# First feed-forward block of a hybrid decoder step: fourteen tiles as paired block products, eight as plain tiles

## The chip, the cores and the metric

The kernel runs on one core of a Trainium2 chip. The metric is the device time of one execution in microseconds; 520 token columns (512 prompt positions and 8 new tokens) go through the whole trunk in one launch. TensorE (PE) multiplies, ScalarE (ACT), VectorE (DVE) and GpSimd (POOL) work on the data around it, SyncE (SP) issues most of the transfers.

## The reference, cut to what matters

The trunk has two layers. Each adds half a SwiGLU feed-forward block, then a mixer, then half a feed-forward block again. The mixer of layer 0 is a diagonal state-space layer (S5), that of layer 1 a latent attention.

```
D_MODEL = 1024; SEQ = 512; DEC_BATCH = 8; D_FF = 2816; FFN_RES = 0.5
def swiglu(x, w_gate, w_up, w_down):
    return (jax.nn.silu(x @ w_gate) * (x @ w_up)) @ w_down
x = x + FFN_RES * swiglu(rmsnorm(x, ffn_norm[layer, 0]), ffn_w_gate[layer, 0], ffn_w_up[layer, 0], ffn_w_down[layer, 0])
...
    dt = jnp.exp(log_dt)[:, None]; mag = jnp.exp(dt * a_re)          # S5: lambda, B and C from parameters alone
    lam_re, lam_im = mag * jnp.cos(dt * a_im), mag * jnp.sin(dt * a_im)
    ...                                                              # powers of lambda times B and C feed the scan
```

The change is in the very first feed-forward block (called ffn00) and in the preparation of the S5 parameters, which runs beside it.

## The kernel before, in words

Activations lie transposed: 8 blocks of 128 channels by 520 columns. Every fp32 operand is split into a high and a low fp32r part (`wh`, `wl` for weights, `xh`, `xl` for the input), and a product takes three passes: high by high, low by high, high by low. A matrix instruction has 260 columns, so a weight block of 128x128 costs six instructions. The 2816 hidden features are 22 tiles of 128.

**ffn00** is written plainly (`ffn_first` on each engine). Eleven tiles are done: for each tile a gate product and an up product (`product`, line 2377; 8 channel blocks, 48 instructions each), evicted by DVE with the row scale (lines 1903 and 1907), gated with ACT's sigmoid and two DVE multiplications, and split into `h0` by ACT (L1218) and DVE (L1914). Then eight down products over these 11 tiles (66 instructions each) are added to `x` by DVE (L1924). Then the same again for the other eleven tiles, "half 1". Each weight slot is loaded by SP (`load`, L762) into one of two buffers `raw`, copied to `wh` by ACT (`his`, L990), and the rest taken by DVE (`los`, L1579). A load of slot n is issued once `los` of slot n-2 is done. Each queue takes its work strictly in the order written.

**The other three feed-forward blocks** (`seven` on each engine, planned by class `Seven`) do four tiles plainly and the other eighteen in pairs. A pair of tiles against two halves of the channels and two halves of the columns is a 2x2 block product, done with seven products in place of eight (L2487; each is 12 instructions for gate and 12 for up, so 168 for a pair, against 192 for its two tiles done plainly). It needs sums of weight blocks (DVE, L1680 to L1697), sums of input blocks (`xof`, split into `xoh`, `xol`), and extra copies out of and into PSUM by ACT. The pairs lie in groups `GROUPS = ((0,1,2,3),(4,5,6,7),(8,9,10))`; after each group come eight down products over its tiles (`down`, L2459), which need the last pair's hidden values in order (`z_hl`).

**The S5 preparation** lies beside ffn00. Lambda is made by POOL at the start. PE spreads it over channels with `param_rows` after tile 3, `b_rows` (matrix instructions and turns) after tile 10, `c_columns` in the first down products. DVE then does `lambda_columns` (L1946) and `input_matrix` (L1955 to L1959) at the first down product of half 0, one `input_power` (L1969 to L1973) in each of tiles 12 to 18, and one `output_power` (L1992 to L2001) in each of the last down products. After the last input power (`s_bp`) POOL makes powers of lambda (`mu`, L3390 to L3408), writes zeros to DRAM (L3417, waits until they have landed) and, once ACT has written `bp` to DRAM (L1229, 4 MB, at the first down product of half 1), gathers it back turned as `wsh` (L3422, 4 MB, 512-byte pieces). SP, in order behind its weight loads, loads the carried state (L828, four small transfers); PE turns it after the sixth of the last eight down products and waits for it there (`s_s0`). `wsh` is first read some 7 us after the block ends (L2771).

Of the kernel before, what the change touches and what calls it, by code (L numbers as in the profile page):

```python
# [27 lines left out]
P = 128  # L28
# [72 lines left out]
TOGETHER = NF // 2 - PLAIN  # L101
# [5 lines left out]
NSS = len(S_STEPS)  # L107
AFTER_CH = 2 * NPG * (R + DR) - (NQT + 2 * RT) * TOK
# [60 lines left out]
def plan():  # L169
    s = Slots()  # L170

    for _ in range(2):
# [19 lines left out]

class Seven:


    def __init__(self, then):
        self.kind, self.load, self.done, self.loads = [], [], [], []
        self.start, self.down = {}, {}
        for c, group in enumerate(GROUPS):
            for p in group:  # L200
                self.start[p] = len(self.kind)
                if p < PLAIN:
                    for f in (2 * p, 2 * p + 1):
# [32 lines left out]
    def counts(self):  # L236

        r, k = TOGETHER, len(self.loads)
        return {"in": (self.landed(k - 1 if (k - 1) % 2 == 0 else k - 2), self.landed(k - 1 if (k - 1) % 2 else k - 2)),
                "hi": self.n, "lo": self.n, "used": self.done[-1], "up": KD * (len(GROUPS) - 1),  # L240
                "xh": 7, "xl": 7, "xf": 5, "ev": 4 * PLAIN, "ps": 2 * PLAIN, "ph": 2 * PLAIN, "hh": NF // 2, "hl": NF,
# [15 lines left out]
def yoco_step(nc, inp, out):  # L257
    slots = plan()
    total = len(slots.nk)
    SEV = {"ffn01": Seven(True), "ffn10": Seven(True), "ffn11": Seven(False)}  # L260
    at = slots.at
    AFTER = {"ffn01": at["kv"], "ffn10": at["dq"], "ffn11": total}
    ctx = ExitStack()
    with ctx:
# [34 lines left out]
        with ExitStack() as s:  # L299
            bp, tmpc, lamc = take(s, ("bp", [P, KD, L, 2, NS], F32), ("tmpc", [P, 2, 2, KD * NS], F32),  # L300
                                  ("lamc", [P, 2, KD, NS], F32))
            with ExitStack() as a:
                xin, xsin, grow = take(a, ("xin", [P, 4, D], F32), ("xsin", [NB, D], F32),
                                       ("grow", [P, P], F32))
            with ExitStack() as a:
                h0, = take(a, ("h0", [P, 2 * HF, TOK], F32R))
# [59 lines left out]
        sums_at = {"ffn01": (sum_1, sum_2), "ffn10": (sum_1, sum_3), "ffn11": (sum_1, sum_2)}  # L366
# [22 lines left out]
        bnat = tmpc[:, 0].rearrange("p r (n c) -> p r n c", c=GC)  # L389
        lam, lam_l, fac = prm(8, 2), prm(2, 2), prm(10, 2)  # L390
        lam_r, lam_i, fac_r, fac_i = (prm(8 + i) for i in range(4))
        hfirst = (h0[:, 0:HF, :], h0[:, HF:2 * HF, :])

        def plane(j):
# [4 lines left out]
            ("s5_u_rows", (KD, P // GC, GC, L, NCH)), ("s5_w_rows", (KD, P // GC, GC, L, 2 * NS))))  # L399
        dr_us, dr_k = (nc.dram_tensor(n, shape, F32).ap() for n, shape in (  # L400
# [75 lines left out]
        r_out, R_0 = [s_in, p_in], [64, 48]  # L476
# [4 lines left out]
        z_in, IN_0 = x_in[0:2], 16  # L481
        z_hi, z_lo, z_used, z_up, z_xh, z_xl, z_xf = s_u, s_z, s_w, s_y1, s_yp, s_ysp, s_ct
        z_ev, z_ps, z_ph, z_hh, z_hl, z_sum, z_add = s_ls, s_bb, s_bp, s_sn, s_tp, s_e, s_xe
        z_seed, z_p5, z_u2, z_sg, z_h = s_ctc, s_sb, s_wb, s_x, s_sc
        now = {"hi": 8, "lo": 2, "used": 4, "up": 1, "xh": 4, "xl": 1, "xf": 2, "ev": 1, "ps": 1, "ph": 1, "hh": 2, "hl": 4, "sum": 11,
               "add": 9, "seed": 8, "p5": 2, "u2": 1, "sg": 16, "h": 8, "in": (IN_0, IN_0)}
        ZB = {}
        for f_, sv_ in SEV.items():
# [7 lines left out]
        HID = {"ffn00": 0, "ffn01": NF, "ffn10": 2 * NF, "ffn11": 3 * NF}  # L496
# [4 lines left out]
        NEXT = {"ffn01": "kv", "ffn10": "mla"}  # L501
        XN = {"glu": 0}
# [25 lines left out]
        def raw_of(name, n):  # L528
# [3 lines left out]
            if sv.kind[n][0] == "down":  # L532
                _, c, d = sv.kind[n]
                k = 2 * len(GROUPS[c])
# [21 lines left out]
        def as_slot(name, buf, n):  # L556
# [4 lines left out]
            k = KD if kind[0] == "plain" else 2 * len(GROUPS[kind[1]])  # L561
# [16 lines left out]
        def hid(name, c):  # L578

            if c == LAST and name in NEXT:  # L580
                return [t[:, 0:len(GROUPS[c])].rearrange("p i k t -> p (i k t)").rearrange("p (f c) -> p f c", c=TOK) for t in (xoh, xol)]
            return xh, xl

        PREPARE = {"ffn01": {2: 1, 3: 2, 4: 3, 5: 4}, "ffn10": {0: 1, 1: 2, 3: 3, 4: 4}, "ffn11": {2: 1, 3: 2, 4: 3, 5: 4}}
# [2907 lines left out]
```

## Time and profile before

| | |
|---|---|
| median of 3 runs | 2012.95 us (2010.68 to 2013.16) |
| span of the profiled execution | 2007.1 us |
| PE busy | 1960.4 us (98%), 17604 instructions |
| DVE busy | 1277.0 us (64%) |
| ACT busy | 820.4 us (41%) |
| POOL busy | 132.8 us (7%) |
| DMA | 211.55 MB, mean 105 GB/s |
| ffn00, first matrix instruction to the last update of x | 12.0 to 418.7 us |
| S5 mixer to its first output product | 418.7 to 481 us |

The profile shows one execution. The median of the timed runs is 5.85 us above its span; sums are made on the span and carried over to the median by that distance. Times are microseconds from the start of the span. In the page's 40 slices of 50 us PE is at 8 or 9 tenths throughout, the granted TensorE clock at 9 tenths or more.

### The profile page before, as it was taken

To read this page: it belongs to the slowest core of one execution; us is meant where nothing else is said; L and a number is where in the kernel's file an instruction comes from. 1 tells how busy PE (TensorE), PEld (TensorE's weight loads), DVE (VectorE), ACT (ScalarE), POOL (GpSimd) and SP (SyncE) were. 2 spreads that over 40 slices of the span, in tenths; PEclk is the share of its full clock that TensorE was granted. 3 is DMA by queue.
4 is the path that set the end of the run, shared out by engine and by line. 5 is a ranking of instruction groups with operands and counts; after the bars stand their busy time and mean duration, and the time that the engine had idled before them with its cause. 6 is when DMAs were issued, how large, how long until landed. Compare 5 with 4: busy or idle time off the path is not lost.

```text
span 2007.1 us, 41612 instructions
## 1 busy us (share of the span) xinstructions
PE 1960.4 (98%) x17604; PEld 1875.2 (93%) x17604; DVE 1277.0 (64%) x1771; ACT 820.4 (41%) x1243; POOL 132.8 (7%) x231
## 2 busy tenths in 40 slices
PE   8999999988999999999999999999989999999999
PEld 7999999987999999999999999997666799999998
DVE  6445486697469577576884856655764349668474
ACT  5332233343245244255452534454654244345252
POOL 3002002010000000000000000000047000000000
PEclk9999999989999999999999999999999999999999
DMA  7233234864342322234322322231248422323222
GB/s 151 84 102 88 75 93 115 269 140 100 95 137 85 120 89 95 77 105 116 97 85 85 127 85 86 84 101 51 54 119 231 149 71 83 127 85 120 91 74 75
DMA packets 260624, 211.55 MB, mean 105 GB/s; under 512 B 42372, under 2 KB 235426, under 8 KB 260450
## 3 DMA queue, kind: packets, MB, share of 16 engines
q1 hardware_dynamic: 248528, 187.52, 31.9%
q0 software_dynamic: 6656, 13.69, 2.4%
q10 hardware_dynamic: 5266, 7.85, 1.2%
q8 instruction: 130, 2.13, 0.4%
q14 instruction: 44, 0.36, 0.1%
HBM read 195.29 MB, written 10.33 MB: 102 GB/s over the span
## 4 chain that ended last, share of the span: by engine, by line
PE 67%; DVE 3%; ACT 2%; issue 2%; SPq 1%; DMA 1%; DVEq 0%; ACTq 0%
PE ps L2459 25%; PE ps L2487 25%; PE ps L2388 6%; PE ps L2401 2%; PE ps L2947 1%; PE ps L3053 1%; PE ps L3209 1%; PE ps L3086 1%; SPq L654 1%; SPq L639 1%; DMA cb<-cache_ckv 1%; PE ps L2841 1%; PE ps L3030 1%; DVE wl L1668 0%; DVE xl L1619 0%
## 5 line engine op out<-in xcount | busy, mean ns | idle before, releaser
L2388 PE MATMUL ps<-xh,wh 128*128 128x260 f32 x1088 | 286.9, 285 | 2.6 <-DVE xl L1619 1.4
L2388 PE MATMUL ps<-xl,wh 128*128 128x260 f32 x1088 | 283.7, 283 | 0.0
L2487 PE MATMUL ps<-xoh,wh 128*128 128x260 f32 x992 | 281.3, 284 | 1.3 <-DVE sq L1835 1.3
L2487 PE MATMUL ps<-xoh,wl 128*128 128x260 f32 x992 | 281.0, 283 | 0.0
L2487 PE MATMUL ps<-xol,wh 128*128 128x260 f32 x992 | 280.6, 283 | 0.0
L2459 PE MATMUL ps<-xh,wh 128*128 128x260 f32 x872 | 228.8, 284 | 0.6 <-DVE wl L1668 0.6
L1067 ACT ACTIVATE wh<-rw 128x1024 fp32r<-128x1024 f32 (+1 forms) x135 | 138.8, 1029 | 218.6 <-PE ps L2459 151.7
L2459 PE MATMUL ps<-xl,wh 128*128 128x260 f32 x872 | 227.0, 282 | 0.0
L2388 PE MATMUL ps<-xh,wl 128*128 128x260 f32 x1088 | 219.3, 283 | 0.0
L990 ACT ACTIVATE wh<-raw 128x1024 fp32r<-128x1024 f32 (+1 forms) x90 | 100.4, 1116 | 283.4 <-PE ps L2388 250.5
L2388 PEld LDWEIGHTS ps<-xh,wh 128*128 128x128 f32 x1088 | 205.6, 189 | 6.9 <-issue 3.9
L2388 PEld LDWEIGHTS ps<-xl,wh 128*128 128x128 f32 x1088 | 205.1, 188 | 0.0
L1668 DVE TENSOR_TENSOR wl<-rw,wh 128x1024 fp32r<-128x1024 f32 (+1 forms) x135 | 160.3, 1188 | 67.3 <-ACT wh L1067 67.2
L2487 PE MATMUL ps<-xoh,third 128*128 128x260 f32 x1040 | 198.6, 283 | 0.6 <-DVE sq L1835 0.6
L2487 PEld LDWEIGHTS ps<-xoh,wh 128*128 128x128 f32 x992 | 186.6, 188 | 1.6 <-DVE wl L1668 1.6
L2487 PEld LDWEIGHTS ps<-xol,wh 128*128 128x128 f32 x992 | 186.9, 188 | 0.0
L2487 PEld LDWEIGHTS ps<-xoh,wl 128*128 128x128 f32 x992 | 186.8, 188 | 0.0
L1579 DVE TENSOR_TENSOR wl<-raw,wh 128x1024 fp32r<-128x1024 f32 (+1 forms) x92 | 120.5, 1310 | 89.5 <-ACT wh L990 81.8
L2459 PE MATMUL ps<-xh,wl 128*128 128x260 f32 x872 | 175.5, 283 | 0.0
L2388 PEld LDWEIGHTS ps<-xh,wl 128*128 128x128 f32 x1088 | 167.9, 189 | 0.0
L2459 PEld LDWEIGHTS ps<-xh,wh 128*128 128x128 f32 x872 | 164.4, 189 | 1.7 <-DVE wl L1668 1.1
L2487 PEld LDWEIGHTS ps<-xoh,third 128*128 128x128 f32 x1040 | 164.8, 188 | 0.8 <-DVE third L1668 0.8
(550 smaller groups left out, 4202.2 us busy)
## 6 DMA issues: line engine op xcount, KB each, us to landing
rw<-ffn_w_gate SPq DMA_DIRECT2D x33, 1024.0 KB, 5.4
rw<-ffn_w_up SPq DMA_DIRECT2D x33, 1024.0 KB, 8.0
rw<-ffn_w_down SPq DMA_DIRECT2D x12, 2048.0 KB, 7.8
raw<-ffn_w_gate SPq DMA_DIRECT2D x22, 512.0 KB, 3.9
raw<-ffn_w_up SPq DMA_DIRECT2D x22, 512.0 KB, 3.9
raw<-ffn_w_down SPq DMA_DIRECT2D x16, 704.0 KB, 4.8
rw<-ffn_w_down SPq DMA_DIRECT2D x6, 1536.0 KB, 6.7
cb<-cache_ckv SPq DMA_DIRECT2D x72, 128.0 KB, 3.7
```

What stands on the lines that cost most here:

```text
L639: eng.dma_start(kb[j][:, g, :], inp["cache_kpe"][bass.ds(numbers[b][g], 1)].rearrange("a p r -> p (a r)")).then_inc(arrived[j], 16)
L654: eng.dma_start(cb[j][:, g, :], inp["cache_ckv"][bass.ds(numbers[b][g], 1)].rearrange("a p r -> p (a r)")).then_inc(arrived[j], 16)
L990: run(wh[par_][:, 0:size], raw[par_][:, 0:size], ACT.Copy).then_inc(w_hi, 1)
L1067: run(as_slot(name, slot_h(name, n), n), raw_of(name, n), ACT.Copy).then_inc(z_hi, 1)
L1579: tt(wl[par_][:, 0:size], raw[par_][:, 0:size], wh[par_][:, 0:size], ALU.subtract).then_inc(w_lo, 1)
L1668: tt(as_slot(name, slot_l(name, n), n), raw_of(name, n), as_slot(name, slot_h(name, n), n), ALU.subtract).then_inc(z_lo, 1)
L2388: got = mm(ps[0:width, bank + half, 0:HALF], w[par_][:, k * width:k * width + width], src[:, k0 + k, half * HALF:half * HALF + HALF], star ...
L2401: return nc.tensor.transpose(dst, src, ident[0:rows, 0:rows])
L2459: got = mm(ps[:, bank + half, T0], w[:, cols], src_[:, k, half * HALF:half * HALF + HALF], start=first and m == 0 and s == 0, stop=last an ...
L2487: got = mm(ps[:, bank + mat, T0], w[:, cols], src[:, j, k, :], start=first and k == 0 and m == 0 and s == 0, stop=k == 3 and m == 1, skip_ ...
L2841: got = mm(ps[:, bank + half, 0:HALF], w[slot][:, k * P:k * P + P], src[:, k, half * HALF:half * HALF + HALF], start=k == 0 and m == 0 and ...
L2947: got = mm(ps[:, 2 * (i % 2) + half, 0:HALF], cols, src[:, k, half * HALF:half * HALF + HALF], start=k == 0 and o == 0 and s == 0, stop=k ...
```

## The change

Only ffn00 and the S5 preparation change. Its first fourteen tiles now go through `seven`: tile 0 as before (`opening`), tiles 1 to 3 plainly, tiles 4 to 13 as five pairs in groups `((0,1,2),(3,4),(5,6))`, each followed by its eight down products. The last eight tiles (`SINGLE`) stay plain, with one set of eight down products. The hidden values of the first two groups are kept in `xh`, `xl`, where the input was; so POOL writes both to DRAM at the start and reads them back after the second group. That block has semaphores of its own (`ZS`, borrowed from later stages, which then wait for a count higher by `ONCE`).

The S5 preparation moves: `param_rows` into the third group's down products, `b_rows` between the gate and the up product of the first plain tile, `lambda_columns` and `input_matrix` into that tile on DVE, `input_power(f)` into plain tiles 1 to 7, `c_columns` after the third plain tile. The order in the last eight down products is as it was, with 8 tiles (48 instructions, 512 KB of weights each) where there were 11 (66 instructions, 704 KB).

```
-        for _ in range(2 * HF):
-            s.add("ffn00", KD)
-        for _ in range(KD):
-            s.add("ffn00", HF)
+    for _ in range(2 * (1 + SINGLE)):
+        s.add("ffn00", KD)
+    for _ in range(KD):
+        s.add("ffn00", SINGLE)
...
+GROUPS_FIRST = ((0, 1, 2), (3, 4), (5, 6))
+SINGLE = NF - 2 * sum(len(g) for g in GROUPS_FIRST)
...
+    SEV = {"ffn00": Seven(True, GROUPS_FIRST, 1), "ffn01": Seven(True), "ffn10": Seven(True), "ffn11": Seven(False)}
...
+            pool.wait_ge(xl_rdy, GEN["ffn00"] + KD)
+            for t, dst in zip((xh, xl), dr_x):
+                pool.dma_start(dst, t[:, :, :]).then_inc(x_kept, 16)
+            pool.wait_ge(x_kept, 32)
+            pool.wait_ge(ZS["ffn00"].used, ZB["ffn00"]["used"] + SEV["ffn00"].done[SEV["ffn00"].down[LAST - 1] + KD - 1])
+            for t, src in zip((xh, xl), dr_x):
+                pool.dma_start(t[:, :, :], src).then_inc(x_kept, 16)
...
+                seven("ffn00")
+                los(3)
+                for f in range(SINGLE):
+                    n, j = 2 + 2 * f, f % 2
+                    dve.wait_ge(w_used, n + 1)
+                    tt(halves(ta[:, j, :]), banks(0), halves(rbc[:, :]), ALU.mult).then_inc(f_g, 1)
+                    los(n + 2)
+                    if f == 0:
+                        lambda_columns()
+                        input_matrix()
+                    dve.wait_ge(w_used, n + 2)
...
+                    if f >= 1:
+                        input_power(f)
...
+                seven("ffn00")
+                pe.wait_ge(x_kept, 64)
+                pe.wait_ge(s_z, 1)
+                for f in range(SINGLE):
+                    n = 2 + 2 * f
+                    if f > 0:
+                        pe.wait_ge(f_g, f)
+                    product(n, 0, KD, X, 0)
+                    if f == 0:
+                        pe.wait_ge(x_upd, UPD["half"] + KD)
+                        b_rows()
+                    else:
+                        pe.wait_ge(f_u, f)
+                    product(n + 1, 1, KD, X, 2)
+                    if f == 2:
+                        c_columns()
```

The order on DVE where `lambda_columns` (`lst`) and `input_matrix` (`tmpc`, `bp`) stand. Before, behind the last tile of half 0 and ahead of the first update of `x`:

```order
L1914 TENSOR_TENSOR h<-ta,h 128x520 [waits f_hi]
L1946 TENSOR_SCALAR lst<-ps 64x32 [waits s5_param_ps]
L1946 TENSOR_SCALAR lst<-ps 64x32 x19
L1955 TENSOR_TENSOR tmpc<-bp,ps 128x1024 [waits s5_param_sb]
L1955 TENSOR_TENSOR tmpc<-bp,ps 128x1024
L1958 TENSOR_TENSOR bp<-tmpc 128x8x64 [waits s5_bb]
L1959 TENSOR_TENSOR bp<-tmpc 128x8x64
L1924 SCALAR_TENSOR_TENSOR x<-ps,x 128x520 [waits w_used,dch]
```

Now, in the first plain tile, between the eviction of its gate (`ta<-ps`) and that of its up product (`sq<-ps`):

```order
L1935 TENSOR_TENSOR ta<-ps,rbc 128x520 [waits w_used]
L1605 TENSOR_TENSOR wl<-raw,wh 128x1024 [waits w_hi]
L1979 TENSOR_SCALAR lst<-ps 64x32 [waits s5_param_ps]
L1979 TENSOR_SCALAR lst<-ps 64x32 x19
L1988 TENSOR_TENSOR tmpc<-fac_rows,ps 128x1024 [waits s5_param_sb]
L1988 TENSOR_TENSOR tmpc<-fac_rows,ps 128x1024
L1991 TENSOR_TENSOR bp<-tmpc 128x8x64 [waits s5_bb]
L1992 TENSOR_TENSOR bp<-tmpc 128x8x64
L1941 TENSOR_TENSOR sq<-ps,rbc 128x520 [waits w_used,dch]
L1943 TENSOR_TENSOR ta<-ta,tb 128x520 [waits f_sig]
L1945 TENSOR_TENSOR ta<-ta,sq 128x520 [waits f_t]
L1605 TENSOR_TENSOR wl<-raw,wh 128x1024 [waits w_hi]
```

The up product's eviction and the next up weights' low part now stand behind the whole of it.

The end of the block on DVE. Before, three tiles without a power lay between the last input power (lines 1969 to 1973) and the first update; the last tile ended so:

```order
L1911 TENSOR_TENSOR ta<-ta,sq 128x520 [waits f_t]
L1579 TENSOR_TENSOR wl<-raw,wh 128x1408 [waits w_hi]
L1914 TENSOR_TENSOR h<-ta,h 128x520 [waits f_hi]
L1924 SCALAR_TENSOR_TENSOR x<-ps,x 128x520 [waits w_used]
L1579 TENSOR_TENSOR wl<-raw,wh 128x1408 [waits w_hi]
L1992 TENSOR_TENSOR tmpc<-lst,cT 128x512 [waits s5_param_sb]
```

Now the last input power stands right ahead of the first update:

```order
L1948 TENSOR_TENSOR h<-ta,h 128x520 [waits f_hi]
L2002 TENSOR_TENSOR tmpc<-lamc,bp 128x1024 [waits s5_param_ps]
L2003 TENSOR_TENSOR tmpc<-lamc,bp 128x512
L2004 TENSOR_TENSOR tmpc<-lamc,bp 128x512
L2005 TENSOR_TENSOR bp<-tmpc 128x8x64 [waits dch]
L2006 TENSOR_TENSOR bp<-tmpc 128x8x64
L1955 SCALAR_TENSOR_TENSOR x<-ps,x 128x520 [waits w_used]
L1605 TENSOR_TENSOR wl<-raw,wh 128x1024 [waits w_hi]
L2025 TENSOR_TENSOR tmpc<-lst,cT 128x512 [waits s5_param_sb,s5_bp]
```

All that waits for it (`s5_bp`: the 4 MB write by ACT, POOL's powers and its gather) starts beside the down products and no longer three tiles ahead of them.

On SP the end of the block keeps its order (weights of the down products, then the carried state); only the weights are smaller:

```order
L771 DMA raw<-ffn_w_down 128x8x128 [waits w_lo] x8
L844 DMA tb<-state_s_re 128x128 [waits f_lo]
L844 DMA tb<-state_s_re 128x128
L844 DMA tb<-state_s_im 128x128 x2
L771 DMA raw<-s_w_glu_v 128x8x128 [waits w_lo]
```

## Rows read from the trace of the kernel before

**Rows 1.** The page, busy time of each engine: us, share of the span, instructions.

```profile
PE 1960.4 (98%) x17604; PEld 1875.2 (93%) x17604; DVE 1277.0 (64%) x1771; ACT 820.4 (41%) x1243; POOL 132.8 (7%) x231
```

**Rows 2.** Waits of PE from 30 to 370 us: total, times, longest.

```profile
PE ps L2414 <- DVE rstd L1605: 0.5, 1, 0.5
```

**Rows 3.** Chain that ended last: start, length, what, instructions; second feed-forward block.

```profile
664.71 46.03 PE ps L2459 x384
710.75 81.03 PE ps L2487 x672
```

**Rows 4.** Waits of PE from 571 to 700 us.

```profile
PE ps L2487 <- DVE sq L1835: 0.6, 1, 0.6
```

**Rows 5.** Timeline of DVE at the end of a group, second block: start, length.

```profile
898.74 0.42 DVE L1747 SCALAR_TENSOR_TENSOR sq<-ps,sq 128x260 f32<-128x260 f32 x1
...
900.30 1.31 DVE L1704 TENSOR_TENSOR xol<-sq,xoh 128x520 fp32r<-128x520 f32 x2 [1.14 <-ACT xoh L1085]
```

**Rows 6.** Timeline of ACT at the same place.

```profile
899.19 1.07 ACT L1085 ACTIVATE xoh<-sq 128x1040 fp32r<-128x1040 f32 x1 [1.64 <-DVE sq L1747]
```

**Rows 7.** Timeline of PE, `b_rows`, first and last of its 38 instructions.

```profile
153.53 1.89 PE L2710 MATMUL ps<-cst,be 128*128 128x64 f32 x16
...
157.14 0.52 PE L2401 MATMUL ps<-cst,cT 64*64 64x64 f32 x6
```

**Rows 8.** Timeline of DVE there: `lambda_columns`, end of `input_matrix`, next weights.

```profile
157.83 2.54 DVE L1946 TENSOR_SCALAR lst<-ps 64x32 f32<-64x32 f32 x20
...
167.57 0.70 DVE L1924 SCALAR_TENSOR_TENSOR x<-ps,x 128x520 f32<-128x520 f32 x1
168.19 2.61 DVE L1579 TENSOR_TENSOR wl<-raw,wh 128x1408 fp32r<-128x1408 f32 x1
```

**Rows 9.** Timeline of DVE, tile with the last power to the block's end.

```profile
315.11 0.70 DVE L1907 TENSOR_TENSOR sq<-ps,rbc 128x520 f32<-128x520 f32 x1 [2.19 <-PE ps L2388]
...
321.88 0.69 DVE L1973 TENSOR_TENSOR bp<-tmpc 128x512 f32<-128x512 f32 x1
...
349.63 0.70 DVE L1907 TENSOR_TENSOR sq<-ps,rbc 128x520 f32<-128x520 f32 x1 [2.65 <-PE ps L2388]
...
360.58 1.29 DVE L1992 TENSOR_TENSOR tmpc<-lst,cT 128x512 f32<-128x512 f32 x2
...
363.71 0.69 DVE L2001 TENSOR_TENSOR ctcw<-tmpc 128x512 f32<-128x512 f32 x1
...
418.04 0.70 DVE L1924 SCALAR_TENSOR_TENSOR x<-ps,x 128x520 f32<-128x520 f32 x1
```

**Rows 10.** Timeline of POOL: start chain's end, powers' start, zeros, gather.

```profile
42.87 0.28 POOL L3355 TENSOR_TENSOR cT<-cT 64x64 f32<-64x64 f32 x1
...
322.63 0.29 POOL L3390 COPY mu<-lst 128x128 f32<-128x128 f32 x1 [147.20 <-DVE bp L1973]
...
337.61 1.01 POOL L3417 DMA_DIRECT2D s_tap_rows<-kpT  x1 [0.30 <-POOL kpT L3415]
...
371.39 2.76 POOL L3422 DMA_DIRECT2D wsh<-s_w_rows  x1 [32.77 <-DMA s_w_rows<-bp]
```

**Rows 11.** DMA issues at 334 to 345, 360 to 368, 368 to 376: size, us to landing.

```profile
s_tap_rows<-kpT POOLq DMA_DIRECT2D x1, 448.0 KB, 3.9
...
raw<-ffn_w_down SPq DMA_DIRECT2D x1, 704.0 KB, 14.2
...
wsh<-s_w_rows POOLq DMA_DIRECT2D x1, 4096.0 KB, 23.3
```

**Rows 12.** Tile `raw` from 340 to 425 us: landing times of the down weights.

```profile
DMA to landing us min/median/max: 4.6/5.0/18.2
```

**Rows 13.** Timeline of SP: a down load, then the carried state.

```profile
377.97 0.37 SPq L762 DMA_DIRECT2D raw<-ffn_w_down  x1
...
385.98 9.42 SPq L828 DMA_DIRECT2D tb<-state_s_re  x2
...
395.44 0.91 SPq L828 DMA_DIRECT2D tb<-state_s_im  x2
```

**Rows 14.** Timeline of PE: the turns of the carried state.

```profile
399.24 0.66 PE L2401 MATMUL ps<-cst,tb 128*128 128x128 f32 x4
```

More of the change, by code:

```diff
@@ L12 @@
 import math
+from collections import namedtuple
 from contextlib import ExitStack
@@ L190, in plan, with __init__ @@
     return s
+Signals = namedtuple("Signals", "arrived hi lo used up xh xl xf ev ps ph hh hl sum add seed p5 u2 sg h")
 class Seven:
-    def __init__(self, then):
+    def __init__(self, then, groups=GROUPS, before=0):
         self.kind, self.load, self.done, self.loads = [], [], [], []
         self.start, self.down = {}, {}
-        for c, group in enumerate(GROUPS):
+        self.groups, self.pairs, self.skip = groups, sum(len(g) for g in groups), 2 * before
+        self.tiles = {p: [f for f in (2 * p, 2 * p + 1) if f >= before] for p in range(PLAIN)}
+        for c, group in enumerate(groups):
             for p in group:
@@ L202, in __init__ @@
                 if p < PLAIN:
-                    for f in (2 * p, 2 * p + 1):
+                    for f in self.tiles[p]:
                         for mat in range(2):
@@ L1744, in left_over @@
-                    tt(g[:, :, T1_], g[:, :, T1_], u, ALU.mult).then_inc(z_h, 1)
-                    dve.wait_ge(z_sg, Z["sg"] + 3 * r + 3)
-                    dve.wait_ge(z_used, Z["used"] + sv.done[sv.start[p] + 6])
-                    stt(g[:, 1, T0], ps[:, C_B + 1, T0], -1.0, g[:, 1, T0], ALU.mult, ALU.mult).then_inc(z_h, 1)
-                begins = {sv.start[p]: p for p in range(PLAIN + 1, NF // 2)}
+                    dve.wait_ge(z.sg, Z["sg"] + 3 * r + 2)
+                    dve.wait_ge(z.add, Z["add"] + 4 * r + 4)
@@ L1751, in ahead @@
+                    tt(g[:, :, T1_], g[:, :, T1_], u, ALU.mult).then_inc(z.h, 1)
+                    dve.wait_ge(z.sg, Z["sg"] + 3 * r + 3)
+                    dve.wait_ge(z.used, Z["used"] + sv.done[sv.start[p] + 6])
+                    stt(g[:, 1, T0], ps[:, C_B + 1, T0], -1.0, g[:, 1, T0], ALU.mult, ALU.mult).then_inc(z.h, 1)
+                begins = {sv.start[p]: p for p in range(PLAIN + 1, sv.pairs)}
                 def ahead(n):
@@ L1756, in ahead @@
                         second_sum(begins[n + 3])
-                seven_lo(name, 1)
+                if not sv.skip:
+                    seven_lo(name, 1)
                 if name in NORM:
-                    rms_row(name, lambda: seven_lo(name, 2))
-                for c, group in enumerate(GROUPS):
-                    apart = c == LAST and name in NEXT
+                    rms_row(name, lambda: seven_lo(name, 2 - sv.skip))
+                for c, group in enumerate(sv.groups):
+                    apart = c == LAST and name in APART
                     for p in group:
@@ L1868, in seven @@
                             los(AFTER[name])
+                        if apart and name not in NEXT:
+                            continue
                         if apart:
@@ L2477, in plain @@
                             each(k)
-                    got.then_inc(z_used, 1)
+                    got.then_inc(z.used, 1)
                 def seventh(p, j, mat, bank, first):
@@ L2501, in down @@
                             result(d - 1)
-                    got.then_inc(z_used, 1)
+                    got.then_inc(z.used, 1)
                 def result(d):
```

645 lines of the change are left out of this document (312 added, 333 removed).

## The prediction

> **What bounds the kernel now.** I read the page first: PE is busy for 1960.4 of 2007.1 us [rows 1], so only fewer matrix instructions, or PE standing idle somewhere new, can move the time. Then the waits of PE: from 30 to 370 us, nearly the whole first block, it waits 0.5 us in all [rows 2]. The first block is therefore a pure stream of matrix instructions, and every instruction less counts fully until some other engine or a transfer is late. Third, the chain through the second block, which already works in pairs: 384 plain instructions take 46.03 us and 672 paired ones 81.03 us [rows 3], so 0.1199 us a plain and 0.1206 us a paired instruction. Last, I looked for what is nearly late at the end of the block, since there the same S5 work is now to lie beside a third less matrix work.
>
> **Part 1, fewer instructions.** Five pairs are 5 x 168 = 840 paired instructions in place of 960 plain ones: 840 x 0.1206 - 960 x 0.1199 = 101.3 - 115.1 = **-13.8 us**. The down products are 22 x 48 = 1056 instructions either way, however they are grouped.
>
> **Part 2, entering the pairs.** The second block waits 0.6 us once for DVE's additions there [rows 4]; the same code runs here: **+0.6**, between 0 and 2.
>
> **Part 3, short groups.** The third instruction block of a group's first down product needs the hidden values of the last pair. After the last paired instruction DVE starts its multiplication at 898.74 [rows 5], ACT's copy runs from 899.19 to 900.26 [rows 6], DVE's rest of the first half is ready about 0.7 us after 900.30 [rows 5]: 2.4 us after 898.57, where that group's instructions ended (the multiplication starts 0.17 us later). A group of three tile pairs has 4 x 6 instructions, 2.9 us, ahead of that need, so it is hidden; the two groups of two pairs have 2 x 6, 1.4 us. That is 1.0 us each, **+2.0** (0 to 4). In those groups a down product is 24 instructions, 2.9 us; ACT's and DVE's copies for it are half the size of those in 5.75 us, so they fit.
>
> **Part 4, the parameters in the first plain tile.** `b_rows` takes PE 153.53 to 157.66, 4.1 us [rows 7], before and after, so nothing. But DVE's `lambda_columns` and `input_matrix` take 157.83 to 167.57, 9.7 us [rows 8]. Before, they lay beside a 7.9 us down product that nobody hurried. Now PE has the up product and the next gate product ahead, 96 x 0.1199 = 11.5 us from the end of `b_rows`, until it needs the next up weights, whose low part stands behind all that on DVE. From the end of `b_rows`: 10.0 us, then eviction and two multiplications at 0.7 each, then the low part, 1.2 us and up to 1 more, since the one in this place took 2.61 us against the 1.6 us of its kind while POOL worked [rows 8]. That is 14.5 us, so PE waits 3.0: **+3.0** (1 to 5). The later tiles have 11.5 us for about 10.3 of DVE, as now; the backlog is worked off in two tiles.
>
> **Part 5, keeping the input.** POOL issues the write of 4.26 MB when its parameter chain ends at 43.2 [rows 10]; ACT wants it done when the plain tiles end, near 27 + 7.3 products of 5.75 = 69 us. A 4.19 MB gather in 512-byte pieces took 23.3 us on the same queue [rows 11]; in long rows it can't be slower, so it lands by 67. The read back has the whole third group, 63 us of PE. Cost 0; if the write were late, up to 5 us.
>
> **Part 6, the end of the block.** Call D the start of the last eight down products (349.6 before [rows 9]). Before, the tail from D to the last update of x, 418.7 [rows 9], was 69.1 us, of it 528 x 0.1199 = 63.3 us of matrix work. Now it has 384 instructions, 46.0 us. DVE has less slack: its last power ends 7.4 us after the up product's end (315.1 to 322.6 [rows 9]), so its list starts at D + 7.4; then 8 x (0.7 + 1.2) for updates and weights, seven output powers at 3.8 (360.58 to 364.40 [rows 9]) and 2.7 for the last half power: 52 us. One stall comes on top: the weights of the fifth down product are requested at D + 9.4, just as ACT's 4 MB write runs; the load in that place took 14.2 us to land [rows 11] against 5.0 usually [rows 12], here about 12.6 (smaller), which holds DVE for 3 us, of which it had used up 0 to 2. So the last update ends near D + 53.5: an overhead over the matrix work of 7.5 us where it was 5.8: **+1.7** (0 to 5).
>
> Sum: -13.8 + 0.6 + 2.0 + 3.0 + 1.7 = **-6.5 us**. The profiled execution would have a span of 2000.6, the median 2012.95 - 6.5 = 2006.5 us. Adding up the ends of these terms gives -13 to +2.
>
> **Rival 1: the carried state comes behind the gather, and the kernel is slower.** SP loads the carried state behind the down weights, PE waits for it after the sixth down product. Before, POOL issued its 4 MB gather at 371.39 [rows 10], D + 21.8, and it landed 23.3 us later, at 394.7 [rows 11]. A down load issued at 377.97 [rows 13], behind it, landed only 18.2 us later [rows 12], at 396.2; SP was held for 9 us at the first state load and got the last one out at 396.3 [rows 13]; PE turned the state at 399.24 [rows 14], without a wait, but D + 49.6. Now PE comes there at D + 37.5, twelve us earlier, while the gather is issued later: last power D + 7.4, POOL's powers 15.0 (322.63 to 337.61 [rows 10]) and more under a busy DVE, zeros 3.9 to land [rows 11], so D + 27 at the earliest, D + 30 likely. The eighth weights go out at D + 30 and the state right behind. If the gather's packets are ahead of them, they land as it ends, near D + 50; PE stands 12 us; then two down products and one and a half powers on DVE put the last update at D + 64.6, 11.1 us over my forecast: +4.6, **2017.5 us** (2012 to 2021, the upper part if the granted clock falls in the pause). For it: the landing times of [rows 12, 13]. Against it: the load issued 3 us ahead of the gather was not held so long, and the gather took some us from its issue until it crowded the others out. The point that decides: with the gather issued before D + 28 the state is late, after D + 30 it slips through.
>
> The Trainium skill ("DMA: Bandwidth & Descriptors", section "Queues, rings and completion order") says each transfer engine goes round the queues it has work for, a packet from each in turn. By that rule the small-packet loads of SP would finish with the gather and not before it, which is this rival and its 2017.5 us; the 18.2 us of [rows 12] agrees.
>
> **Rival 2: only the multiplications count.** If the third and fourth parts cost nothing and DVE keeps up in the tail, -12 us: **2001 us**. For it: PE never waited for these in the second block beyond 0.6 us [rows 4]. Against it: 14.5 against 11.5 us in part 4.
>
> **Rival 3: the gain is given back in pieces.** Ends of parts 3, 4 and 6 together, or the state late by 4 to 8 us: -3 to +2 us, **2012.5 us**. For it: before, the state had some 0.5 us to spare. That the change does not do what it says has little room: the pairs use the code of the other blocks.
>
> **How the numbers follow.** Forecast 0.48 (own range 2003 to 2010), rival 1 0.25, rival 3 0.20, rival 2 0.07. About 0.2% (4 us) is what a measurement of this kernel can tell from no change. Faster than 2008.9: rival 2 and most of the forecast, 0.50. Within: the forecast's end, rival 3 and the low part of rival 1, 0.28. Slower than 2017: 0.22. The range 2001 to 2019 leaves out one in six or so. Forecast and rival 1 are the two hills; the sign hangs on a race of a few microseconds between POOL and SP.
>
> **What the changed profile would show.** PE with 120 matrix instructions less. A wait of PE for DVE near 3 us in the first plain tile, and waits of about 1 us at the start of the second and third group's down products. ACT never waiting for the written input. In the tail, the time from the first down product to the last update, 53.5 us; a state wait of PE behind the sixth product, none for the forecast, some 12 us for rival 1, and then SP held at the state load. I am wrong if PE waits in the pairs themselves, if the weights' loads at the start are late (3 MB more are requested at once there), or if the S5 mixer after the block starts later than 7 us behind the last update because its rows are loaded beside the gather.

## The result, and the profile after

The changed kernel is slower: 2026.98 us, median of 4 runs (2023.77 to 2032.62), against 2011.82 us for the kernel before, run beside it; ratio 1.0086, 95% interval 1.0069 to 1.0103. Run once more later it took 2024.76 us, ratio 1.0065 (1.0043 to 1.0087). The forecast of 2006.5 us had the wrong sign, and the time lies above the range of 2001 to 2019, and above the upper end that rival 1 was given (2021). The profiled execution is the slowest of the four; its span is 2030.9 us, 23.8 over that of before, where the medians differ by 15.2. The second run's profiled execution has a span of 2023.4, 16.3 over.

The page answers [rows 1]: PE has 120 instructions less, as it should, yet is busy 2.2 us longer. The granted clock (PEclk, tenths of full speed, 40 slices of 50.8 us) is down in two slices, 406 to 508 us; before, the lowest slice was at 8 tenths (one slice, at 401 to 452 us; the section on the time before says 9 or more).

```profile
PE 1962.6 (97%) x17484; PEld 1873.2 (92%) x17484; DVE 1339.3 (66%) x1848; ACT 856.4 (42%) x1310; POOL 141.5 (7%) x235
...
PEclk9999999977999999999999999999999999999999
```

The waits of PE (total, times, longest) in 35 to 255, 255 to 310 and 362 to 420 us stand against the single 0.5 us of [rows 2]: the two short groups (1.0 us each), the first plain tile (6.2 us), and in the tail the carried state (14.1 us).

```profile
PE ps L2492 <- DVE xol L1730: 1.0, 1, 1.0
PE ps L2492 <- DVE xl L1730: 1.0, 1, 1.0
```

```profile
PE ps L2421 <- DVE wl L1605: 6.2, 1, 6.2
```

```profile
PE ps L2434 <- DMA tb<-state_s_im: 14.1, 1, 14.1
PE ps L2440 <- ACT sq L1031: 1.4, 1, 1.4
PE ps L2421 <- DVE wl L1605: 0.4, 1, 0.4
```

The chain of work that ended last (start, length, what) shows both pauses from the inside. First the pairs, at the price of [rows 3] (40.53 / 336 = 0.1206 us); then the first plain tile, where DVE holds the chain from 268 to 286 us; then the tail, where the state does, and the 48 instructions behind it take 8.15 us where 48 x 0.1199 = 5.75 would be usual.

```profile
90.26 34.57 PE ps L2492 x288
124.82 40.53 PE ps L2520 x336
```

```profile
275.21 2.42 DVE bp L1992
277.63 0.02 issue
277.65 0.70 DVE sq L1941
278.35 1.61 DVE ta L1943
279.96 0.02 issue
279.99 2.72 DVE ta L1945
282.71 3.29 DVE wl L1605
286.00 0.14 issue
286.14 13.94 PE ps L2421 x95
```

```profile
401.98 15.93 DMA tb<-state_s_im
417.96 1.11 PE ps L2434 x4
...
419.66 8.15 PE ps L2421 x48
```

Where the 23.8 us are, D being the start of the last eight down products as in the prediction:

| stretch | before | after | forecast for after |
|---|---|---|---|
| start to D | 349.6 | 365.3 | 358.7 |
| D to the start of the last update of x | 68.4 | 69.6 | 52.8 |
| from there to the next block's first product | 76.2 | 79.9 | as before |
| from there to the end | 1512.9 | 1516.1 | as before |

(Before D the change has 24 instructions more in all: 144 of the tail's now come earlier. The prediction's 53.5 us run to the end of the last update, which is 0.7 us long; here and below its start is meant, hence 52.8.) The last row is not the change's doing: the second run of the same kernel took 1513.1 us there. So three stretches are to be explained: 6.6 us in the first, 16.8 in the second, 3.7 in the third.

### The profile page after: what moved, and what is told of

The parts are those of the page before. It is cut to its first block, busy times and chain, and to the rows that moved or that the text cites. A ratio compares the mean times of both kernels' runs of the same rounds, so it can differ in the third digit from the quotient of the medians.

```text
span 2030.9 us, 41470 instructions
## 1 busy us (share of the span) xinstructions
PE 1962.6 (97%) x17484; PEld 1873.2 (92%) x17484; DVE 1339.3 (66%) x1848; ACT 856.4 (42%) x1310; POOL 141.5 (7%) x235
## 4 chain that ended last, share of the span: by engine, by line
PE 83%; DVE 7%; ACT 3%; issue 3%; SPq 2%; DMA 2%; ACTq 0%; DVEq 0%
PE ps L2492 31%; PE ps L2520 29%; PE ps L2421 11%; PE ps L2434 2%; SPq L663 1%; PE ps L2973 1%; PE ps L3079 1%; PE ps L3235 1%; PE ps L3112 1%; SPq L648 1%; DMA tb<-state_s_im 1%; DMA raw<-ffn_w_down 1%; DVE stmp L707 1%; DVE wl L1605 1%; PE ps L3056 1%
## 5 line engine op out<-in xcount | busy, mean ns | idle before, releaser
L1082 ACT ACTIVATE wh<-rw 128x1024 fp32r<-128x1024 f32 (+2 forms) x169 | 169.1, 1001 | 280.1 <-PE ps L2492 197.4
L2492 PE MATMUL ps<-xh,wh 128*128 128x260 f32 x1048 | 275.0, 283 | 1.6 <-DVE xl L1730 1.0
L2492 PE MATMUL ps<-xl,wh 128*128 128x260 f32 x1048 | 272.8, 282 | 0.0
L1694 DVE TENSOR_TENSOR wl<-rw,wh 128x1024 fp32r<-128x1024 f32 (+2 forms) x169 | 194.8, 1153 | 84.9 <-ACT wh L1082 84.7
L2492 PE MATMUL ps<-xh,wl 128*128 128x260 f32 x1048 | 211.0, 283 | 0.0
L2492 PEld LDWEIGHTS ps<-xh,wh 128*128 128x128 f32 x1048 | 197.6, 189 | 2.9 <-DVE xl L1730 1.2
L1892 DVE SCALAR_TENSOR_TENSOR x<-ps,x 128x520 f32<-128x520 f32 x96 | 67.1, 699 | 185.4 <-PE ps L2492 185.4
L2421 PE MATMUL ps<-xh,wh 128*128 128x260 f32 x672 | 179.9, 289 | 8.9 <-DVE wl L1605 6.2
L2421 PE MATMUL ps<-xl,wh 128*128 128x260 f32 x672 | 176.8, 285 | 0.0
L2520 PE MATMUL ps<-xol,third 128*128 128x260 f32 x616 | 174.1, 283 | 0.0
L2492 PE MATMUL ps<-xh,third 128*128 128x260 f32 x912 | 169.7, 283 | 0.0
L1082 ACT ACTIVATE third<-rw 128x1024 fp32r<-128x1024 f32 (+2 forms) x85 | 86.2, 1014 | 136.9 <-PE ps L2492 96.3
```

Of the source, the lines that this page charges most:

```text
L1082: run(as_slot(name, slot_h(name, n), n), raw_of(name, n), ACT.Copy).then_inc(z.hi, 1)
L1694: tt(as_slot(name, slot_l(name, n), n), raw_of(name, n), as_slot(name, slot_h(name, n), n), ALU.subtract).then_inc(z.lo, 1)
L1892: done = stt(xd, banks(bank), 0.5, xd, ALU.mult, ALU.add)
L2421: got = mm(ps[0:width, bank + half, 0:HALF], w[par_][:, k * width:k * width + width], src[:, k0 + k, half * HALF:half * HALF + HALF], star ...
L2492: got = mm(ps[:, bank + half, T0], w[:, cols], src_[:, k, half * HALF:half * HALF + HALF], start=first and m == 0 and s == 0, stop=last an ...
L2520: got = mm(ps[:, bank + mat, T0], w[:, cols], src[:, j, k, :], start=first and k == 0 and m == 0 and s == 0, stop=k == 3 and m == 1, skip_ ...
```

## The experiments

The theory after the traces: the multiplications gain what was said, and two pauses give it back: POOL's products beside DVE's list in the first plain tile, and the 4 MB gather ahead of what SP loads for the tail; each pause is followed by PE products at the lower clock (1.2 for 2.4 GHz; the granted clock is 0.50 from 286 to 290 us and from 410 to 420 us). Rivals: DVE's list is slow of itself; the state's transfer is slow of itself; the gain of the pairs cannot be had in so short a tail, since its transfers have to pass anyway. The milestones of each kernel's profiled execution, in us, and its time:

| kernel | D | tail | last update to S5 chunks | next block | median | ratio to before (95%) |
|---|---|---|---|---|---|---|
| before | 349.6 | 68.4 | 11.9 | 494.2 | 2010.6 to 2011.8 | 1 |
| changed | 365.3 | 69.6 | 15.1 | 514.8 | 2027.0 | 1.0086 (1.0069 to 1.0103) |
| changed, again | 364.8 | 67.8 | 13.3 | 510.4 | 2024.8 | 1.0065 (1.0043 to 1.0087) |
| state_early | 364.1 | 67.9 | 11.9 | 508.3 | 2025.7 | 1.0076 (1.0046 to 1.0106) |
| gather_behind | 364.6 | 55.5 | 17.7 | 502.3 | 2018.8 | 1.0040 (1.0026 to 1.0053) |
| tail_mended | 364.6 | 55.6 | 19.2 | 503.8 | 2019.4 | 1.0039 (1.0026 to 1.0052) |
| pool_after | 360.0 | 68.3 | 13.1 | 505.7 | 2021.1 | 1.0050 (1.0036 to 1.0063) |
| sums_later | 360.4 | 69.1 | 12.7 | 506.6 | 2023.8 | 1.0052 (1.0030 to 1.0074) |
| pool_split | 358.0 | 67.8 | 13.1 | 503.3 | 2019.3 | 1.0045 (1.0022 to 1.0068) |
| busy_wait | 365.4 | 66.7 | 12.4 | 509.1 | 2025.5 | 1.0081 (1.0056 to 1.0105) |
| all_four | 360.5 | 55.6 | 18.9 | 499.9 | 2016.3 | 1.0024 (1.0012 to 1.0036) |
| halves_all | 361.0 | 61.0 | 13.2 | 501.1 | 2014.5 | 1.0021 (1.0003 to 1.0038) |
| mended | 357.3 | 52.6 | 13.5 | 487.9 | 2002.8 | 0.9957 (0.9941 to 0.9974) |

(Tail: D to the start of the last update. S5 chunks: DVE's first `stmp` operation. From it to the next block it is 64 to 66 us everywhere. What follows the start of the next block is the same work in all of them, and took between 1511.7 and 1517.6 us in the profiled executions; so a few us between two of these executions can come from outside the table's stretches.)

**The state alone, `state_early`.** SP, in `ffn_first`, behind the second down load:

```diff
+                    if d == 1:
+                        sp.wait_ge(f_lo, SINGLE - 1)
+                        ... the four loads of s0r
...
-            for r, nm_ in enumerate(("re", "im")):
-                for j in range(2):
-                    sp.dma_start(s0r[:, 2 * r + j, :], ...
```

> The changed kernel, but SP loads the carried state behind the second of the last eight down weights, some 20 us ahead of the 4 MB gather, and not behind the eighth. D is the start of the last eight down products; in the changed kernel the last update of x stood at D + 69.6. Theory, the gather holds every load that is issued near it: the 14.1 us wait for the state goes, but the eighth down weights, issued in the same stretch (at D + 32), are as late, so PE waits some 10 us ahead of its eighth down product instead; the last update comes near D + 62 and the kernel is 5 to 9 us shorter than the changed one, about 2019. Rival, the state's own transfer of small pieces is the slow one: no wait in the tail, last update near D + 54, 14 to 18 us shorter, about 2011.

The tail is 67.9 us, hardly shorter, and the time, 2025.7 us, is that of the changed kernel and not the expected 2019. The wait only has another name. Waits of PE and of ACT from 385 us on:

```profile
PE ps L2442 <- ACT sq L1033: 10.4, 2, 8.9
```

```profile
ACT wh L1008 <- DMA raw<-ffn_w_down: 22.5, 2, 14.8
```

PE waits for the squares of the sixth column block, which stand on ACT behind the copy of the eighth down weights, and these have not landed (ACT's longer wait, 14.8 us; the shorter one is for the fifth weights, loaded beside ACT's 4 MB write). The theory was right that they are as late as the state; it expected 5 to 9 us, and less than 2 came. Rival "the state's own transfer" is out.

**The gather behind the state, `gather_behind`,** is one line on POOL, ahead of the gather:

```diff
             pool.wait_ge(r_w, RW_0 + 16)
+            pool.wait_ge(s_s0, 64)
             pool.dma_start(wsh...
```

> The changed kernel, but POOL issues its 4 MB gather only when the carried state has landed (D + 38 to D + 41 in place of D + 29). Theory, the gather is what holds the state and the eighth down weights: PE waits 0 to 3 us at the state and for nothing else in the tail, its clock stays at full speed there, the last update comes near D + 56 in place of D + 69.6; the gather lands near D + 63, just ahead of its first use, and the rows of the S5 inputs are loaded beside it, which costs 0 to 5 us in the S5 stage. 10 to 15 us shorter than the changed kernel, 2012 to 2017. Rival, the crowding only moves on: the S5 stage waits for its rows or for the gather, the kernel gains under 5 us, above 2022.

Tail 55.5 us, no wait of PE there over 1.4 us, and 8 us shorter than the changed kernel. That is less than the 10 to 15 us expected: 2018.8 us for 2012 to 2017. The landing times say why; the last number is the median from issue to landing, for issues in 396 to 402 us in the changed kernel, then in 385 to 405 us in this one:

```profile
wsh<-s_w_rows POOLq DMA_DIRECT2D x1, 4096.0 KB, 22.7
raw<-ffn_w_down SPq DMA_DIRECT2D x1, 512.0 KB, 20.2
...
tb<-state_s_re SPq DMA_DIRECT2D x2, 64.0 KB, 18.3
tb<-state_s_im SPq DMA_DIRECT2D x2, 64.0 KB, 16.5
```

```profile
raw<-ffn_w_down SPq DMA_DIRECT2D x2, 512.0 KB, 4.8
...
tb<-state_s_re SPq DMA_DIRECT2D x2, 64.0 KB, 3.9
tb<-state_s_im SPq DMA_DIRECT2D x2, 64.0 KB, 3.6
```

In the changed kernel the gather had been issued at 394.30 us, the eighth weights at 396.95 and the state from 397.36 on, and all landed as the gather ended, between 415 and 418 us.

```profile
394.30 2.76 POOL L3456 DMA_DIRECT2D wsh<-s_w_rows  x1 [3.55 <-DMA s_tap_rows<-kpT]
396.95 0.37 SPq L771 DMA_DIRECT2D raw<-ffn_w_down  x1
397.36 2.02 SPq L844 DMA_DIRECT2D tb<-state_s_re  x2
```

The theory's third part, a price in the S5 stage, holds too, and is a little above its range of 0 to 5 us (5.8 us ahead of the S5 chunks, against the kernel before): the gather, now issued at 402.6, lands 4.9 us behind the last update and the S5 chunks start 17.7 us behind it instead of 11.9. `tail_mended` does both, with POOL waiting until the eighth weights are copied:

> The changed kernel with the tail alone mended: the carried state is loaded behind the second of the last down weights, and POOL issues the whole gather only when the eighth down weights are in use (copied by ACT). Theory: no wait of PE over 1 us for a transfer in the tail, last update of x at D + 53.5 to D + 55.5 (D + 69.6 in the changed kernel), the gather lands near D + 60 and costs the S5 stage 3 to 7 us as it did where it waited for the state (82 us from the last update to the next block, 75.5 before the change). 2017 to 2020, as with that kernel. Rival, the gather's place does not matter for the S5 stage and its length there was chance of the clock: 76 us, 2012.

It is the same kernel in time (2019.39 us), with 19.2 us to the chunks: the gather's place decides in the S5 stage as well, and the rival is out.

**POOL beside DVE, `pool_after` and `sums_later`.** The first lets POOL start its six products when DVE has written the second tile's low up weights; the second moves two of DVE's own operations, the sums of the input matrix, behind the low up weights that PE waits for, to the end of the first plain tile.

```diff
             pool.wait_ge(s_e, 2)
+            pool.wait_ge(w_lo, 6)
```

```diff
                     tt(h0[:, SINGLE + f, :], ...).then_inc(f_lo, 1)
+                    if f == 0:
+                        input_sums()
```

> The changed kernel, but POOL starts its six products of the S5 preparation only when DVE has finished the second tile's low up weights. Theory, POOL's work beside slows DVE's operations there (0.7 us ones took 1.7 and 2.7, the low weights 3.4 in place of 1.2): DVE's list from the end of the b_rows products takes 14 in place of 17.8 us, PE waits 2 to 3 us in place of 6.2, its clock falls for a shorter time or not at all; 3 to 7 us shorter than the changed kernel, 2020 to 2024. Rival, DVE is slow there because of its own reads from PSUM and broadcasts: PE waits 6 us as before and the time is 2027.

> The changed kernel, but DVE forms the two sums of the S5 input matrix (4.5 us there with POOL beside it) at the end of the first plain tile, behind the low up weights that PE waits for, not ahead of them. Theory, PE waits for the length of DVE's list: 6.2 - 4.5, about 1.5 to 3 us left, and the clock falls little; the moved 2 us are hidden in the next tiles' slack (11.5 us of PE for 10.3 of DVE), or come back as a wait of at most 2 us in the second tile. 4 to 7 us shorter than the changed kernel, 2020 to 2023. Rival, the slack of the next tiles is too small and the wait only moves on: PE waits as much in the second or third tile, 2027.

DVE's same four operations in the changed kernel are in the chain above (0.70, 1.61, 2.72, 3.29 us). In `pool_after` its timeline has

```profile
273.99 0.70 DVE L1941 TENSOR_TENSOR sq<-ps,rbc 128x520 f32<-128x520 f32 x1
274.61 0.69 DVE L1943 TENSOR_TENSOR ta<-ta,tb 128x520 f32<-128x520 f32 x1
275.33 0.70 DVE L1945 TENSOR_TENSOR ta<-ta,sq 128x520 f32<-128x520 f32 x1
275.95 1.22 DVE L1605 TENSOR_TENSOR wl<-raw,wh 128x1024 fp32r<-128x1024 f32 x1
...
286.88 2.79 DVE L1945 TENSOR_TENSOR ta<-ta,sq 128x520 f32<-128x520 f32 x1
289.59 3.40 DVE L1605 TENSOR_TENSOR wl<-raw,wh 128x1024 fp32r<-128x1024 f32 x1
```

Without POOL, the list ends 9.5 us behind the `b_rows` products instead of 17.8, and PE does not wait in this tile at all. The same operations are slow one tile later (the last two rows), where POOL now works, and there PE waits 2.3 us. D comes 5.3 us earlier, in the expected range, but the expected 14 us for the list was far off: the operations are as slow as POOL makes them, not by themselves. The Trainium skill ("SBUF — State Buffer", section "Who interferes with whom") says that a VectorE instruction with two inputs in SBUF contends with a GpSimd instruction that reads SBUF, and one with at most one such input does not, outside VectorE's two-port modes. The trace agrees: in the changed kernel `sq<-ps,rbc`, with an input in PSUM, took 0.70 us from 277.65 on, beside this product of POOL, as it did alone.

```profile
277.15 2.25 POOL L3418 TENSOR_TENSOR cst<-lst,cst 128x1024 f32<-128x1024 f32 x1
```

`sums_later` leaves a wait of 3.0 us, D 4.8 us earlier, and a time just above its expectation.

`pool_split` also holds the last two products back, until the third tile's low up weights (`pool.wait_ge(w_lo, 8)`).

> The changed kernel, but POOL runs the first four of its six S5 products when DVE has finished the low up weights of the second tile, and the other two when it has finished those of the third. Theory, DVE's operations in plain memory are two to four times as long only while POOL works beside them, and PE's pause follows from that: with POOL's products in the stretches in which DVE has little to do, PE waits 0 to 0.5 us from 255 to 310 us (6.2 in the changed kernel, 2.3 one tile later where all six products were held back together), its clock stays at 1.00, and the last eight down products start 9 to 10 us earlier than in the changed kernel. 2016 to 2019. Rival, DVE's list is too long even without POOL: a wait of 2 us or more stays, 2021 as with the products held back together.

The wait is 1.4 us, between the two expectations, and the clock stays at 1.00 there. D is 7.3 us earlier for 9 to 10 expected, the time 2019.3 us for 2016 to 2019. What is left has another cause: DVE's first input power, in the second tile, waits for POOL's last product, with the next weights' low part behind it in DVE's order. Waits of DVE in 255 to 310 us:

```profile
DVE tmpc L2002 <- POOL cst L3422: 4.6, 1, 4.6
```

**What the fallen clock costs, `busy_wait`.**

```diff
                     if d == KD - 3:
+                        for _ in range(16):
+                            mm(ps[:, STATE_BANK, :], ident, x[:, 0, 0:SEQ], ...)
                         pe.wait_ge(s_s0, 64)
```

> The changed kernel, but PE runs 16 idle products (512 columns each, some 14 us, results unused) in the place where it waits for the carried state. Theory, the pause itself costs 14 us and the fallen clock behind it some 3.5 us more: the state comes when it did, the granted clock stays 1.00 up to the last update, which comes at D + 66 in place of D + 69.6; 3 to 5 us shorter than the changed kernel, 2022 to 2024, and the S5 stage keeps or gains a little. Rival, the clock falls for a reason other than the pause: it falls in the same place, no gain, 2027.

Stretches of 10 us (busy us and instructions of PE, PEld, DVE, ACT, POOL, then granted clock, DMA share, GB/s), first the changed kernel, then this one:

```profile
400.00:410.00 10.00, 3.87 (x33) 3.66 (x31) 6.72 (x11) 1.80 (x2) 0.00 (x0) 0.87 1.04 325
410.00:420.00 10.00, 2.04 (x14) 1.32 (x15) 1.74 (x3) 2.70 (x3) 0.00 (x0) 0.50 0.82 228
420.00:430.00 10.00, 10.00 (x72) 9.66 (x72) 6.54 (x10) 2.03 (x3) 5.23 (x5) 0.78 0.37 105
```

```profile
410.00:420.00 10.00, 10.00 (x43) 5.15 (x42) 2.14 (x3) 2.82 (x4) 0.00 (x0) 1.00 0.83 231
420.00:430.00 10.00, 10.00 (x90) 9.66 (x89) 9.32 (x13) 3.78 (x5) 5.21 (x5) 1.00 0.75 184
```

The clock falls because PE stands: with PE occupied it stays at 1.00. But it is worth 1.1 to 2.9 us in the tail (66.7 us against 67.8 and 69.6), and nothing that the times can tell: 2025.5 us, above the 2022 to 2024 expected. In the tail the pause of 14 us was the cost, not what follows it. (The pause in the first plain tile was left as it was.)

**Both places together, `all_four`** (state_early, the late gather, pool_after, sums_later):

> The changed kernel with both places mended: tail as in the run before, POOL's six products after the low up weights of the second tile, and the two sums of the input matrix behind them. Theory, the first plain tile and the tail are two independent losses that add: no wait of PE over 1 us from 255 to 310 us, D some 9 us earlier than in the changed kernel, last update D + 55, S5 stage 80 to 82 us: 2008 to 2012. Rival, what DVE and POOL are spared in the first plain tile they owe at the end of the block (the last power later than D + 7.5, the gather later still): 2014 or more.

The two losses add, as far as the spread lets one see: 3.1 us below `tail_mended` in the median, D 4.1 us earlier. The expected 2008 to 2012 us were not reached: neither kernel alone had gained what was then added. And within the first plain tile the two edits do not add: D is 4.8 us earlier than in the changed kernel (5.3 with `pool_after` alone, 4.8 with `sums_later` alone, 9 expected), and PE still waits 2.5 us, since the moved sums now stand beside POOL's products and take 2.4 us each. The rival's time came, but not its reason: the last power ends at D + 7.4. The kernel is still slower than before, by what stands in the table's fourth column: the late gather, and rows of S5 input loaded beside it (6.4 us median to landing, 19.4 at most, against 3.9 in the kernel before). So the third rival lives: the tail has 17 us less of matrix work, but the change did not shorten the chain of transfers from the last power to S5's first chunk (14.4 us of write, 22.7 of gather).

**The gather in halves, `halves_all`.** First half at once when the rows are written, second when the eighth weights are copied:

> As the run before, but the gather is issued in two halves of 2 MB: the first as soon as its rows are written (near D + 22, ahead of the zeros, where nothing that PE waits for is loaded), the second when the first has landed and the eighth down weights are in use; PE waits for the second half only ahead of its fifth tile of S5 inputs. Theory, no load of the tail is held and the gather is done 8 to 10 us sooner than whole and late: the S5 stage is as long as before the change, 75 to 77 us, last update near D + 55: 2002 to 2007, below the kernel before (2010.6). Rival, the first half holds the seventh or eighth down weights as the whole one did: PE waits 4 to 8 us in the tail, 2008 to 2014.

The rival happened in the tail, though the time is just above its range (2014.5 us for 2008 to 2014). The first half, issued at 385.2, holds the seventh weights, issued at 387.2: ACT waits 7.9 us for them. The other 7.7 us in this line are for the fifth weights, which are loaded beside ACT's write and are as late in `gather_behind`. Waits of ACT from 385 us on:

```profile
ACT wh L1008 <- DMA raw<-ffn_w_down: 15.6, 2, 7.9
```

The tail is 61.0 us, the S5 chunks come in 13.2. Against `all_four`, with the gather whole and late, the halves win 5.7 us ahead of the S5 chunks and lose 5.4 in the tail.

**The write ahead of its time, `mended`.** What had to move was the start of the chain. Five of the eight planes are ready two tiles before the last, so ACT writes them beside the plain tiles, and the gather's first half starts where the write had run (`WRITE_AFTER` is (4, 6), the powers behind which a piece is written; the state and POOL's products are as in `state_early` and `pool_split`):

```diff
                     run(tb[:, f % 2, :], ta[:, f % 2, :], ACT.Sigmoid).then_inc(f_sig, 1)
+                    if f - 1 in WRITE_AFTER:
+                        write_rows(f - 1)
...
             pool.wait_ge(s_bp, 1)
+            pool.wait_ge(r_w, RW_0 + 48)
+            gather(0)
             own(G.tensor_copy(mu...
...
+            pool.wait_ge(w_hi, 2 + 2 * SINGLE + KD)
+            pool.wait_ge(r_wsh, RWSH_0 + 16)
+            gather(4)
```

> The changed kernel with POOL's products split as in the run before, the state loaded early, and the 4 MB of input planes written in three pieces as they are ready (five planes beside the sixth plain tile, two beside the eighth, the last one behind its power) so that the gather's first half can start near D + 11, where the write ran before, and its second half when the eighth down weights are in use, near D + 36. Theory, the gain of the pairs was only hidden by transfers in the wrong place: no wait of PE over 1 us in the tail, last update at D + 55.5 with D near 356, S5 stage 76 to 79 us, next block at 488 to 491 (494.2 before the change): 2004 to 2009, 0.1 to 0.4% below the kernel before. Rival, the same 17 MB of transfers have to pass between the last power and the S5 stage whatever their order: some load is held again (the fourth to sixth down weights behind the first half), PE waits 4 us or more, its clock falls, 2012 to 2016.

2002.8 us, below the changed kernel by 22 us and below the kernel before by 0.43% (0.26 to 0.59), and a little below the 2004 to 2009 expected. D is 357.3, the tail 52.6 us, the next block starts at 487.9. From 370 to 440 us PE waits 3.0 us (less than the rival's 4), and for no transfer; POOL issues the gathers at

```profile
368.63 1.77 POOL L3439 DMA_DIRECT2D wsh<-s_w_rows  x1 [74.96 <-DMA s_w_rows<-bp]
...
395.87 1.69 POOL L3439 DMA_DIRECT2D wsh<-s_w_rows  x1 [4.32 <-DMA s_tap_rows<-kpT]
```

and of the issues of 345 to 410 us the down weights land in 4.7 us median:

```profile
wsh<-s_w_rows POOLq DMA_DIRECT2D x2, 2048.0 KB, 14.0
raw<-ffn_w_down SPq DMA_DIRECT2D x7, 512.0 KB, 4.7
```

That settles the third rival: the volume of the transfers was no bound, their order was. What this kernel does not separate is how much of its last gain is the early write and how much the first half's earlier place: the two were not run apart. The changed kernel itself, run beside it:

> The changed kernel once more, beside the others on this chip: 2023 to 2030.

It came in that range, at 2024.76 us.

## Why the prediction was wrong, point by point

- **Part 1** (-13.8) held: 120 instructions less, 0.1206 us a paired one. **Part 2**: no wait at the entry to the pairs, 0 for 0.6. **Part 3**: 1.0 and 1.0 us as worked out. **Part 5**: ACT never waited for the written input (it landed in 8.1 and 12.4 us) and PE never for it read back. The loads at the start were named as a doubt: the first norm's products start at 32.20 us for 31.38 before, but at 31.89 in the second run and at 31.43 in `mended`, which has the same loads there. A cost of these loads is not shown.
- **Part 4** is the first term that failed. It said 14.5 us for DVE's list and a wait of 3.0, at most 5; the list took 17.8, the wait was 6.2, and the lower clock behind it made 95 instructions last 13.94 us for 11.4: about 9 us for 3. The working had the slow sums and `wl` of [rows 8] in hand, 2.4 for 0.7 us, but priced the two multiplications that follow at their undisturbed 0.7 us (1.7 and 2.7 measured) and the low part at 1.2 and up to 1 more (3.4 measured), though POOL's six products run 14 us, from the end of `lambda_columns` on. (Its terms add up to 14.3 us, not 14.5; that changes nothing.) In the kernel before, only the ones of [rows 8] met them.
- **Part 6, the overhead**, was near where the gather was out of the way: 52.8 us forecast to the start of the last update, 55.5 in `gather_behind`, where the late fifth weights, foreseen, cost PE 1.8 us, 0.4 directly and 1.4 through ACT's squares behind them. `mended` has 52.6, but there the write that makes these weights late lies elsewhere, so the nearness of the two numbers is in part luck.
- **The choice against rival 1** is the step that gave the sign. Its mechanism and place were exact: PE stood 14.1 us (12 said) behind the sixth product, SP was held at the state load. Its deciding point was wrong. "After D + 30 it slips through" took the order of issue for a matter of absolute times; the gather went out at D + 29.0, the eighth weights at D + 31.7 and the state at D + 32.1, and both came in with the gather's end. The argument against, that the gather takes some us until it crowds the others out, rested on a load 3 us *ahead* of it; the load behind it in [rows 12] (18.2 us) was the one that applied.
- **Rival 1's price**, 2017.5 us, was short too. Against the profiled execution it lacks 6.6 us before D, nearly all of it part 4; 5.7 in the tail, where the wait was 14.1 us for 12 and the lower clock, which it kept for the upper end of its range, took 2.4 more; and the S5 stage (1.6 to 3.7). It also priced the state's wait alone; `state_early` shows that the eighth weights would have been next.
- **The S5 stage** was taken as unchanged. It was 3.7 us longer (1.6 in the second run), nearly all of it ahead of the S5 chunks, where the granted clock was 0.66 from 440 to 445 us; in the second run it was 1.00 there. How much of that belongs to the change and how much to the spread between executions of one kernel is open.
- **Rival 2's** condition, no cost in parts 4 and 6, is nearly what `mended` built, and its 2001 us nearly what that took; but that is another kernel than the one predicted.

## What to carry to other kernels

Taking work off the bounding engine shortens every deadline of the transfers beside it; so list what is requested behind the largest transfer in the new order, and treat it as landing with that transfer's end. Where an operation is slow beside POOL in the trace, price all of its kind (here both inputs in SBUF) as slow for as long as POOL works, not only those that happened to meet it. When a large transfer gets in the way, start its chain earlier, in pieces, rather than later: late, it hands part of the loss to the next stage (against the two profiled executions of the changed kernel, `gather_behind` won 12 to 14 us in the tail and lost 3 to 4 ahead of the S5 chunks).

## What the runs showed of the hardware that was not expected

- The 4 MB gather took 22.2 to 23.6 us in all ten kernels that issue it whole, whatever was loaded beside it, while down weights issued 2.7 us behind it (changed kernel) and 6.6 us behind it (before) took 20.2 and 18.2 us, for about 5 where neither it nor ACT's write ran. The queues of the changed kernel from 360 to 440 us (packets, MB, share) show unlike packets, 0.4 KB on the queue that by its volume carries SP's loads, 4 KB on the gather's:

```profile
q1 hardware_dynamic: 15596, 6.39, 31.2%
...
q0 software_dynamic: 1168, 4.65, 19.9%
```

  The Trainium skill ("DMA: Bandwidth & Descriptors", section "Queues, rings and completion order") has each engine take a packet from each queue in turn. By that rule SP's loads get the small share, and the landing times agree.
- DVE operations with both inputs in SBUF took 1.1 to 2.8 us beside POOL's products for 0.7 alone, and 1.9 to 3.4 for 1.2 alone (changed kernel and `pool_after`).
- The granted clock fell to 0.72 in 385 to 390 us of `halves_all`, where PE stood 1.85 us, and stayed at 1.00 in the same stretch of `all_four`, where it stood 1.41 us. What decides between them is open.
